# Two-layer diffusion backbone: the last two expert tiles combined from SBUF, with three reorderings

## The reference, cut to what matters

```python
h = modulate(rms_norm(xp, norm2_g[l]), sh2, sc2)
xp = xp + g2[:, None, :] * moe(h, ...)
# moe
act = jax.nn.silu(gate) * up * combine[..., None]
return jnp.einsum('tef,efd->td', act, w_down_l)
# diff_attention
lam = jnp.exp(jnp.sum(lp[0] * lp[1])) - jnp.exp(jnp.sum(lp[2] * lp[3])) + lambda_init
```

## Time and profile before

| what | us |
|---|---|
| median of 3 runs | 2059.05 (2053.49 to 2059.27) |
| profiled execution, its own time | 2056.28 |
| its span, first to last instruction | 2054.5 |
| mean granted TensorE clock | 0.976 |

### The profile page before, as it was taken

The page is one execution under the profiler, slowest core; times in us unless marked ns, Lnnn a source line. Parts: engine busy times, 40 slices in busy tenths (PEclk is TensorE's granted clock), DMA queues, the critical chain, the costliest instruction groups (busy, mean ns, idle before and its releaser), DMA issues. The chain is left out here.

```text
span 2054.5 us, 31276 instructions
## 1 busy us (share of the span) xinstructions
PE 1912.6 (93%) x12731; PEld 1617.7 (79%) x12731; DVE 1080.4 (53%) x1766; ACT 884.8 (43%) x1423; POOL 314.5 (15%) x120
## 2 busy tenths in 40 slices
PE   6999999999999979999779998898999998899993
PEld 4899866699999857777578997677999987577762
DVE  4385367641433256777573734665243334577763
ACT  4443455532222235566454435555222233466653
POOL 1303100032224120000111121000212331000003
PEclk9999999999999999999979999999999999999996
DMA  7422477725612159999441220002222222999954
GB/s 262 131 62 64 147 247 256 240 88 199 211 62 73 47 212 361 315 309 318 156 167 44 75 72 13 1 1 92 89 67 72 73 68 114 376 422 369 311 189 174
DMA packets 163921, 336.34 MB, mean 164 GB/s; under 512 B 10434, under 2 KB 121666, under 8 KB 149316
## 3 DMA queue, kind: packets, MB, share of 16 engines
q1 hardware_dynamic: 151488, 299.63, 41.9%
q0 software_dynamic: 5760, 20.97, 2.7%
q10 hardware_dynamic: 6532, 13.74, 2.1%
HBM read 334.58 MB, written 53.74 MB: 189 GB/s over the span
## 5 line engine op out<-in xcount | busy, mean ns | idle before, releaser
L728 POOL TENSOR_TENSOR wlo<-raw,whi 128x2048 fp32r<-128x2048 f32 x46 | 216.1, 4697 | 1053.2 <-ACT whi L752 1053.2
L2007 DVE TENSOR_TENSOR xw_gu_lo<-xw_gu_raw,xw_gu_hi 128x2048 fp32r<-128x2048 f32 x96 | 218.9, 2284 | 53.7 <-ACT xw_gu_hi L1788 35.6
L171 PE MATMUL psum<-h_hi,whi 128*128 128x320 f32 (+2 forms) x896 | 215.3, 313 | 9.0 <-DVE h_lo L156 6.5
L171 PE MATMUL psum<-h_hi,wlo 128*128 128x320 f32 (+2 forms) x896 | 213.0, 310 | 0.0
L171 PE MATMUL psum<-h_lo,whi 128*128 128x320 f32 (+2 forms) x896 | 213.0, 310 | 0.0
L171 PE MATMUL psum<-whi,h_hi 128*128 128x256 f32 x720 | 210.2, 292 | 0.5 <-ACT v_tok L866 0.5
L171 PE MATMUL psum<-wlo,h_hi 128*128 128x256 f32 x720 | 203.6, 283 | 0.0
L171 PE MATMUL psum<-whi,h_lo 128*128 128x256 f32 x720 | 203.6, 283 | 0.0
L1788 ACT ACTIVATE xw_gu_hi<-xw_gu_raw 128x2048 fp32r<-128x2048 f32 x96 | 178.1, 1907 | 7.6 <-DMA xw_gu_raw<-w_e_up 7.6
L2159 PE MATMUL psum<-xw_d_raw,act_T 128*128 128x512 f32 x400 | 179.9, 592 | 0.9 <-ACT act_T L1818 0.9
L832 ACT ACTIVATE prob<-psum,small_stats 128x640 f32<-128x640 f32 (+1 forms) x160 | 112.0, 705 | 133.1 <-DVE small_stats L1194 133.0
(11 more groups left out here) (319 smaller groups left out, 3657.3 us busy)
## 6 DMA issues: line engine op xcount, KB each, us to landing
xw_d_raw<-w_e_down SPq DMA_DIRECT2D x50, 1024.0 KB, 9.0
xw_gu_raw<-w_e_gate SPq DMA_DIRECT2D x48, 1024.0 KB
xw_gu_raw<-w_e_up SPq DMA_DIRECT2D x48, 1024.0 KB
raw<-w_in SPq DMA_DIRECT2D x46, 1024.0 KB, 5.4
wm_rest<-w_mod SPq DMA_DIRECT2D x40, 1024.0 KB, 5.3
y_rows<-y_sel SPq DMA_DIRECT2D x50, 512.0 KB, 9.5
h_sel<-h_rows SPq DMA_DIRECT2D x48, 512.0 KB, 7.5
h_rows<-c_zero ACTq DMA_DIRECT2D x5, 2560.0 KB, 11.2
```

Source lines behind the costliest of these rows:

```text
L171: mm = pe.matmul(dst, st, mv[q], start=start and n == 0, stop=stop and n == 2)
L728: pool.tensor_tensor(wlo[i % 2][:, :, :], raw[i % 2][:, :, :], whi[i % 2][:, :, :].bitcast(F32), ALU.subtract).then_inc(w_lo, 1)
L2007: dve.tensor_tensor(gu_lo[i % 2][:, n, :, :], gu_raw[i % 2][:, n, :, :], gu_hi[i % 2][:, n, :, :].bitcast(F32), ALU.subtract).then_inc(x_l ...
```

## The change

Four parts. The results of tiles 23 and 24 (overflow tiles 7 and 8) are not stored and gathered again: they stay in `y_sel[1]` and `y_sel[0]`, and each token tile takes its rows from them by matmul with weights `kept_w` (a mark where a choice's row lies in the kept tile, times its combine factor; made by VectorE, turned by TensorE, copied back by VectorE). The gathered rows are weighted and added by matmuls with diagonals of the combine factors (`w_diag`), in the same PSUM group, in place of ScalarE's scale, VectorE's add and the transposes. The gathers wait for the first 23 stores, and rows of kept tiles are redirected to a row of zeros. The next layer's statistics of the first three token tiles, and the fifth tile's squares, move into the expert block; the remainders of the next weights move behind residuals 0 and 1. Lambda moves behind the folds, its exponential to the first z unit. `first_lo(0)` moves behind the scale.

```diff
-        y_ab = [at(f"y_ab{t}", [P, 2, D], (20 + 8 * t) * K if t < 4 else Z + 104 * K) for t in range(TT)]
+        y_ab = [at(f"y_ab{t}", [P, 2, D], off) for t, off in enumerate((28 * K, 40 * K, Z + 104 * K, Z + 80 * K, Z + 88 * K))]
...
+        row_kept = row0(N_TILES - 2)
...
                     def parts_act():
-                        act.activation(sq_e[(TT - 1) % 2][:, :, :], x_T[:, :, (TT - 1) * P:TOK], ACT.Square).then_inc(n1_sq, 1)
...
-                    act.wait_ge(m_l, 2)
-                    act.activation(lam_e[:, :], lam_s[:, :], ACT.Exp).then_inc(m_l, 1)
...
                     for n, u in enumerate(units):
+                        if n == first_z:
+                            act.wait_ge(m_l, 2)
+                            act.activation(lam_e[:, :], lam_s[:, :], ACT.Exp).then_inc(m_l, 1)
...
+                        if first and n == 2:
+                            act.dma_start(y_rows[row_kept:row_kept + 1, :], a["c_zero"][0:1, :]).then_inc(s_rows0, 16)
...
                         dve.tensor_copy(rstd_mix[:, :], flat(3)[:, 0:TOK]).then_inc(n1_rstd, 1)
-                        first_lo(dve, 0)
...
                         scaled_gain(mul1, 8, 0, 0, 4).then_inc(m_done, 1)
+                        first_lo(dve, 0)
...
-                    store_y(N_TILES - 2)
-                    store_y(N_TILES - 1)
...
-                    pool.wait_ge(y_st[0], 16 * ((N_TILES + 1) // 2))
-                    pool.wait_ge(y_st[1], 16 * (N_TILES // 2))
+                    pool.wait_ge(r_st, GATHER_STEPS)
+                    pool.wait_ge(y_st[0], 16 * ((N_TILES - 1) // 2))
+                    pool.wait_ge(y_st[1], 16 * ((N_TILES - 2) // 2))
...
                         std_act(act, 0, e_var)
+                        act.wait_ge(e_sum, TT - 2)
+                        squares_act(act, TT - 1)
...
+                    for h in range(2):
+                        for t in range(TT):
+                            step(dve.tensor_scalar(kept_mark[h][:, t, :], iota_1[:, :], kept_key[:, h, t:t + 1], kept_f[:, h, t:t + 1],
+                                                   ALU.is_equal, ALU.mult))
+                    for s in range(2):
+                        for t in range(TT):
+                            step(dve.tensor_scalar(w_diag[:, s, t, :], ident[:, :], w_ab[:, s, t:t + 1], None, ALU.mult))
...
                     h_low(1)
+                    dve.wait_ge(k_t, KD + 1)
+                    for h in range(2):
+                        dve.tensor_copy(kept_w[h][:, 0:4, :].rearrange("p t s -> p (t s)"), psum[:, 7 - 2 * h, :])
+                    step(dve.tensor_copy(kept_w[0][:, 4, :], psum[:, 6, 0:P]))
+                    step(dve.tensor_copy(kept_w[1][:, 4, :], psum[:, 6, P:2 * P]))
...
+                        if not last and 1 <= t < 3:
+                            next_low(t - 1)
+                        if not last and t == TA + 1:
+                            dve.wait_ge(e_sum, TA)
+                            var_dve(dve, 0, e_var)
+                            rstd_dve(dve, 0, e_var)
...
                     gate_up_first()
+                    pe.wait_ge(r_st, KEPT_STEPS - 2)
+                    for h in range(2):
+                        for t in range(4):
+                            pe.transpose(psum[:, 7 - 2 * h, t * P:(t + 1) * P], kept_mark[h][:, t, :], ident[:, :])
+                    for h in range(2):
+                        mm = pe.transpose(psum[:, 6, h * P:(h + 1) * P], kept_mark[h][:, 4, :], ident[:, :])
+                    mm.then_inc(k_t, 1)
...
                     turn_h(2)
+                    pe.wait_ge(r_st, KEPT_STEPS)
                     down(0)
...
                     for t in range(TT):
-                        pe.wait_ge(m_zb, t + 1)
+                        if not last and t >= 2:
+                            sum_tile(t - 2)
                         if t >= 2:
                             pe.wait_ge(x_step, t - 1)
-                        for f in range(KD):
-                            mm = pe.transpose(flat(t % 2)[:, f * P:(f + 1) * P], y_ab[t][:, 0, f * P:(f + 1) * P], ident[:, :])
+                        for h in range(2):
+                            for f in range(KD):
+                                pe.matmul(flat(t % 2)[:, f * P:(f + 1) * P], y_sel[1 - h][:, f * P:(f + 1) * P], kept_w[h][:, t, :],
+                                          start=(h == 0 and f % 4 == 0), stop=False)
+                        pe.wait_ge(y_ld[t], 32)
+                        for s in range(2):
+                            for f in range(KD):
+                                mm = pe.matmul(flat(t % 2)[:, f * P:(f + 1) * P], y_ab[t][:, s, f * P:(f + 1) * P], w_diag[:, s, t, :],
+                                               start=False, stop=(s == 1 and f % 4 == 3))
                         mm.then_inc(m_zt, 1)
                         if last and t >= 1:
                             turn_x(t - 1)
-                        if not last and t >= 2:
-                            sum_tile(t - 2)
```

More of the change, by code:

```diff
@@ L513, in build @@
         assert 2560 + 320 * 17 + 2560 <= 10592 and 11008 + 4 * P <= 12 * K and Z + 144 * K <= LIMIT
-        y_ab = [at(f"y_ab{t}", [P, 2, D], (20 + 8 * t) * K if t < 4 else Z + 104 * K) for t in range(TT)]
+        y_ab = [at(f"y_ab{t}", [P, 2, D], off) for t, off in enumerate((28 * K, 40 * K, Z + 104 * K, Z + 80 * K, Z + 88 * K))]
+        pos_g = at("rows_gathered", [P, 2, TT], Z + 141 * K + 256, I32)
+        w_diag = at("combine_diag", [P, 2, TT, P], RT + 2560)
+        kept_w = [at(f"kept_tile_w{h}", [P, TT, P], RT + 8000 * h) for h in range(2)]
+        kept_mark = [at(f"kept_tile_marks{h}", [P, TT, P], Z + 32 * K + 2560 * h) for h in range(2)]
+        kept_key, kept_f, kept_r, kept_v = (at(f"kept_{x}", [P, 2, n], RT + 10592 + off) for x, n, off in (
+            ("key", TT, 0), ("factor", TT, 64), ("rows", 2 * TT, 128), ("weights", 2 * TT, 224)))
         sq_e = [at(f"sq_e{i}", [P, KD, P], Z + (112 + 4 * i) * K) for i in range(2)]
@@ L571, in build @@
             "shift_router_step", "shift_logits_ready", "shift_diag_ready", "shift_row_ready", "shift_row_kept"))
-        k_t, k_a, k_d, k_s, k_pk = (sem(x) for x in ("x_gained_turned", "x_gained_kept", "h_tok_ready", "h_rows_written",
+        k_t, k_a, k_d, k_s, k_pk = (sem(x) for x in ("x_gained_or_kept_marks_turned", "x_gained_kept", "h_tok_ready", "h_rows_written",
                                                      "first_rows_marked"))
@@ L591, in row0 @@
             return (n if kind == "s" else NE + n) * P
+        row_kept = row0(N_TILES - 2)
+        assert row0(N_TILES - 1) == row_kept + P and row_kept + 2 * P == SLOTS and (N_TILES - 2) % 2 == 1
         LOGIT_STEPS = 4
@@ L1107, in _ @@
                         dve.tensor_copy(u_mid[:, g, 0:1], u_s[:, 2 * P:2 * P + 1]).then_inc(s_fd, 1)
+                    dve.wait_ge(s_lay, 16 * 5)
+                    dve.tensor_tensor(lam_pr[:, :, :], lam_in[:, :, 0, :], lam_in[:, :, 1, :], ALU.mult).then_inc(m_l, 1)
+                    dve.wait_ge(m_l, 1)
+                    dve.tensor_reduce(lam_s[:, :], lam_pr[:, :, :], AX.X, ALU.add).then_inc(m_l, 1)
+                    dve.tensor_scalar(sub_gain[:, :], sub_raw[:, :], lam_c[:, 1:2], None, ALU.mult).then_inc(m_sg, 1)
                     dve.wait_ge(s_small, 16 * 4)
@@ L1872, in _ @@
                         std_act(act, 0, e_var)
-                    else:
-                        for s in range(TT + 3):
-                            if s + 1 < TT:
-                                scale_a(s + 1)
+                        act.wait_ge(e_sum, TT - 2)
+                        squares_act(act, TT - 1)
+                    else:
+                        for s in range(2, TT + 3):
                             if 2 <= s < TT + 2:
@@ L2050, in _, with next_low @@
                     keep_y(N_TILES - 1)
-                    if not last:
+                    def next_low(c):
                         dve.wait_ge(x_gu, N_TILES)
-                        for c in range(2):
-                            dve.wait_ge(nx_hi, c + 1)
-                            dve.tensor_tensor(wlo[c][:, :, :], raw[c][:, :, :], whi[c][:, :, :].bitcast(F32),
-                                              ALU.subtract).then_inc(nx_lo, 1)
+                        dve.wait_ge(nx_hi, c + 1)
+                        dve.tensor_tensor(wlo[c][:, :, :], raw[c][:, :, :], whi[c][:, :, :].bitcast(F32),
+                                          ALU.subtract).then_inc(nx_lo, 1)
                     for t in range(TT + 4):
-                        if t < TT:
-                            dve.wait_ge(m_za, t + 1)
-                            dve.scalar_tensor_tensor(out=y_ab[t][:, 0, :], in0=y_ab[t][:, 1, :], scalar=w_ab[:, 1, t:t + 1],
-                                                     in1=y_ab[t][:, 0, :], op0=ALU.mult, op1=ALU.add).then_inc(m_zb, 1)
                         if last and 3 <= t < TT + 3:
```

55 lines of the change are left out of this document (29 added, 26 removed).

## The result

The changed kernel took 2078.41 us (median of 4 runs, 2076.86 to 2078.9), the kernel before 2058.94 in the same runs: 1.01 times, 95% interval 1.0082 to 1.0117. It is slower by about 1%, the direction that was forecast and 7 us more than the 2071. The profiled execution took 2078.64 with a span of 2076.9, 22.4 more than the span of before; the medians differ by 19.5. Which steps gave the 22.4 is what the traces are read for.

What follows compares the result with a forecast made beforehand. TensorE, busy 93% of the span, was taken as the bound; +6.5 + 7.4 + 0.3 - 1.3 = +12.9 on 2056.28 made 2069.2, and 2.8 for the median 2071.9, given as 2071; range 2063 to 2079.

Steps and rivals of the forecast that it cites:

- main mechanism: End of both layers: the gathers' round trip is hidden and TensorE's matmuls, 32 per token tile, set the pace.
- rival of late gathers: End of both layers: gathers still wait for something late, about 6 us in each layer, total 2083; chance 0.02.
- no change: Whole kernel: small gains leave +6.8 and run spread gives the rest, 2065, no measurable change; chance 0.09.
- faster: Both tails: new matmuls cost 0.107 us each, 17 us less per layer, total 2038; chance 0.05.
- The price of a matmul: TensorE at both layers' ends: 0.213 us per matmul, 6.81 us per token tile of 32, 1.70 per sum of squares.
- Layer 0's end: Last kept tile to layer 1's projection: +6.5 us, lower end +4.8 with the clock kept high, upper end +8.
- Layer 1's end: Last kept tile to the end: +7.4 us, ends +7.0 and +8.5.
- Routing: Both layers: VectorE's new steps and TensorE's ten transposes lie in existing waits; +0.3 us together, from -4 to +3.
- if the cover goes, 1 to 2 us per layer show: Routing, both layers: 1 to 2 us per layer appear if the waits no longer hide the added work.
- VectorE's share of the forecast: Routing: 8.8 us of new VectorE steps hidden in its scatter waits of 9.71 and 8.45, or 0.3 over in layer 1.
- Slowed scatters: Routing: VectorE's new steps slow four GpSimd issues per layer by 1.1 us each, +8 to +9, total 2080; chance 0.12.
- Start of layer 0: Before the transform: moving lambda behind the folds gives -1.3 us; moving the first remainder gives 0.

Runs made afterwards that it cites:

- e3: The changed kernel without the 16 matmuls per token tile by the two kept tiles, their contribution left out; 2037.32 us, 0.9909 of the kernel before.
- g1: The kernel before, unedited, run again on the same chip as g2; 2055.89 us.
- g2: The changed kernel, unedited, run a third time on the same chip as g1; 2078.27 us.
- h2: The changed kernel with TensorE's matmuls by the kept tiles behind a branch, skipped with this input; 2041.53 us, 0.9926 of the kernel before.
- i1: The changed kernel, unedited, run again on the same chip as i2; 2079.98 us, 1.0101 of the kernel before.
- i2: The kernel before, unedited, run again on the same chip as i1; 2057.29 us.

## Why the prediction was right or wrong

**Direction and main mechanism: right.** TensorE's matmul count replaces the hole and sets the tail; e3 shows it by taking half of the matmuls away. The first gather came 9 us before the last kept tile, TensorE never waited for y_ab, the clock stayed at 1.00. The rival of late gathers fell with that, and "no change" and "faster" with the price.

**The price of a matmul: mis-sized**, 0.213 forecast, 0.2235 measured, because 47 counted records were divided into 5 us without taking off those cut by the edges. It is 0.34 us per token tile and 0.09 per sum: 5 x 0.34 + 3 x 0.09 = 2.0 in layer 0, 1.7 in layer 1.

**Layer 0's end: +6.5 forecast, +8.0 measured** in the first pair, +9.0 on one chip (g1 and g2: 40.4 and 49.3). Residual 4 starts 41.5 after the last kept tile instead of 39.2, which is the price (2.0) and 0.2 before the first matmul. L1430 ran at the high clock, which the forecast had only as its lower end: 2.62 to the projection instead of 3.43. So +2.3 and -0.8 against the forecast's steps.

**Layer 1's end: +7.4 forecast, +9.0 measured.** The turn of residual 3 starts 38.6 after the last kept tile instead of 36.75; the rest is price and the 0.15 ahead of the first matmul. The chain behind it is 0.8 shorter (0.5 forecast).

**Routing: +0.3 forecast, the step that failed.** On one chip it is +2.8 and +2.6 (g1, g2), in the first pair +5.1 and +2.0. The forecast's reasons hold when the semaphore is in time: e3 and h2, with the same routing, take 272.3 to 274.6, the kernel before 272.4 and 273.3. What failed is the term that put TensorE's ten transposes at nothing because they lie in its 2.46 us wait for h_sel: that wait is slack that the kernel before uses up when h_T_first is late, and the trace of before that was read had no such lateness. With it, the ten transposes cost 1.1 us in each layer; on g1 and g2 a stretch of low clock in gate_up(1) adds 1.6 in layer 1, and 1.5 in layer 0 is the copy's later start after the pick product, whose cause is open. The upper end of +3 for both layers was too low; "if the cover goes, 1 to 2 us per layer show" names the right mechanism and the right size for the transposes, but the +0.3 did not count on it. VectorE's share of the forecast held: in layer 0 it still waits 0.3 for the scatters behind its new steps, in layer 1 no longer.

**Slowed scatters: fell.** Issues stay at 0.95 beside L2020 and L2024. Such a lock as the Trainium skill describes for tensor_scalar in a two-port mode (SBUF — State Buffer, section Who interferes with whom) didn't show in these rows; its other sentence, that one SBUF input outside such a mode does not contend, agrees with them. GpSimd's 2.07 us issues again stand beside the same two-input step as before.

**Start of layer 0: -1.3 forecast, -1.4 on one chip (g1, g2), +0.3 on another (i1, i2).** The first agreement is in part luck. Lambda gave about 0.9 there, but the wait it removes is 1.34, 0.73 or nothing in the three traces of before. first_lo was forecast at 0, as whi[1] ends at the same 31.02; it gives 1.0 at the first projection, where TensorE waits for h_lo, and about 0.5 of that is left at the transform. In the first pair it is -2.9, as that trace of before starts 1.3 and 2.4 later than its two repeats.

**The rest of the 22.4:** the first pair has +1.3 between the projection and the second routing: there a stretch of low clock of 3.4 us follows the same 2.52 us wait in the attention that kept the high clock before, and it comes and goes among the traces (679.0 us for this part in the first trace of before, 679.1 to 682.7 in the others). The first pair thus adds up as -2.9 + 5.1 + 8.0 + 1.3 + 2.0 + 9.0 = 22.5. On one chip, g1 and g2, with the semaphore late in both, the same stretches give -1.4 + 2.8 + 9.0 + 0.3 + 2.6 + 9.2 = 22.5, and the spans differ by 22.4.

## What to carry over

Take the price of a matmul from start to start of two groups, never by dividing a window by its count of records. Idle time that an addition is to fill is only free if nothing else is ever late there: ask what the slack absorbs before it is filled. A product that this input doesn't need can be branched around on TensorE, here for 0.9 us a layer, where its first writer and its semaphore stay outside the branch.

## What was not expected of the hardware

A semaphore that comes 2.2 to 4.6 us behind a matmul's last record, in both layers, around ten scatters: in 11 of 18 traces, in all kernels of an experiment's occasion alike, and real in the time (2037.32 and, in one execution, 2046.29 for one program, 2041.53 and 2047.57 for another). It goes by the scatters rather than by the product: ScalarE's copy starts 1.4 to 1.8 us behind the end of the last scatter's issue in 20 of the 22 late layers (the exceptions are layer 0 of g1 and i2, both the kernel before), while its distance from the product's end varies. In the changed kernel's first trace:

```profile
754.97 0.95 POOL L1771 DMA_INDIRECT h_rows<-h_tok,rows_ab  x1 [0.30 <-issue]
```

That issue ends at 755.92, and the copy starts at 757.42. In those traces the scatters' landings are recorded in part only, 80 to 98 of 160 in each layer where the others have 159 or 160. The Trainium skill, Perfetto Trace Analysis, section Tensor Engine Instruction (MATMUL, LD_WEIGHTS), says that the profiler computes a matmul's end from its size and doesn't observe it; so these traces can't tell whether the product itself or only its semaphore is late. Whether the recording of so many events holds TensorE up, or the chip, or something else on those occasions, stays open: nothing that was run changes the recording, and no two of the six occasions shared a chip.
